# A two-block transformer kernel on one core: the second block's residual held as rows, quadrant products with row norms, smaller units and another start in the first block

## The chip, the cores and the metric

The kernel runs on one core of a Trainium2 chip. The metric is the device time of one execution in microseconds (us); smaller is better. A core has a matrix engine (TensorE, in the rows PE, its weight loads PEld), a vector engine (VectorE, DVE), a scalar engine (ScalarE, ACT), GpSimd (POOL) and SyncE (SP), which here issues the transfers of weights. All data are float32. Matrix results land in eight PSUM banks of 128 partitions by 512 values (`bank[0]` to `bank[7]`); everything else lives in SBUF.

## The reference

Two transformer blocks of depth 2 run one after the other on 256 tokens of width 1024.

```python
# first block, each of 2 layers
proj = x @ w_in[l]                       # q, k, v, conv gates cb cc and input cu, qm, branch gates
y_attn = diff_attention(rope(q), rope(k), v, lam, lam_init, diff_subln_g[l])
y_conv = cb * conv3(cc * cu, conv_w[l])  # short_gated_conv
y_mem  = memory_attention(qm, mem, w_mem_kv[l])     # kv = mem @ w_mem_kv
merged = g0*(y_attn @ w_br_attn) + g1*(y_conv @ w_br_conv) + g2*(y_mem @ w_br_mem)
x = layer_norm(ALPHA * x + merged @ w_out[l]);  x = layer_norm(ALPHA * x + grouped_moe(x))

# second block, each of 2 layers; layer 0 updates 256 context tokens too
h = rms_norm(x, g_mix[l]) * (1 + sc1) + sh1          # the same with ctx and its own sc, sh, gt
o = [global_attention, fourier_mix, window_attention](h @ w_in_2[l])
x = x + gt1 * (o @ w_out[l])                         # first output projection
x = x + gt2 * swiglu(rms_norm(x, g_ffn[l]) * (1 + sc2) + sh2, w_gate, w_up, w_down)
return rms_norm(x, g_final)
```

What the change computes in another order are `y_conv @ w_br_conv`, `mem @ w_mem_kv`, the start, and in the second block's layer 0 `o @ w_out`, `... @ w_down`, both gated residual sums and the two root-mean-square norms behind them.

## The kernel before, in words

Each engine has a program of its own, written by hand; semaphores connect them. SP loads weights as tiles of 128 x 4096 values (2 MB) into six slots of `ring`, in the order in which TensorE uses them; a slot is loaded again when TensorE has released it. In SBUF an activation lies mostly as *features* (feature on partition, token along it: `X`, `h2`, `ff`); a *row* layout has tokens on partitions.

**Units.** Several products use seven multiplications of quadrants where a plain product has eight (Strassen's scheme in Winograd's form). A `unit` (before L621) does this for 256 tokens by two weight tiles: TensorE makes seven quadrant products into banks 0 to 6; ScalarE copies the first (`first_product`), VectorE makes the sums of weight quadrants in place in `ring` (`tile_sum`, L1951) and adds the products up. `seven_products` does the same for the second block's layer 0 in feature layout, gate/up (11 units) and down (4 units of 11 by 256 columns), with x in the first 256 columns and the context in the last 256. There `sums_but_last`, `last_sum` and `down_sums` make the weight sums.

**Start.** SP issues x, mem and ctx and then waits for all small parameters (25 transfers that ScalarE's queue issues) before it issues the first weight tile. TensorE waits for all of this too, turns x, mem and ctx into features (48 transposes at L921, copies by ScalarE at L1600), turns the parameters (L925 to L927) and then waits for the sines and cosines that VectorE and ScalarE make (`s_tables`, DVE L2115), before its first product.

**First block, before the attention.** Tiles 0 to 3 (q, k) in features with rope on VectorE, a unit for v, tiles 6 and 7 (conv gates, copied by ScalarE at L1508), tile 8 (conv input), a unit for a branch gate, then `token_blocks(cbT)` (16 matmuls of 512 columns), `tile_features(memT)` (32 of 256 columns) and `token_product(memT)` (16 of 512), and tile qm. Then the attention steps.

**Second block, layer 0, after the attention.** The output projection makes eight feature chunks of 8 matmuls with 512 columns (x and context together). VectorE adds each to `X` with its gate (L2815), ScalarE squares it (L1696), and TensorE adds up the squares with a matrix of constants (`square_step`, `mean_d`), each chunk's one product later. Then the norm: VectorE and ScalarE make the root and its reciprocal for 256 columns of 128 equal rows, VectorE scales (L2424), ScalarE modulates (L1712), and gate/up begins. The down units end in the same kind of chain, into layer 1's first projection (L2379, L1703). In layer 1 the late part already works with rows: `X` is turned back into rows `xt` (L688 on `X`), a diagonal of the gate times a matrix of ones spreads the gate over all rows (`gate_diag`, `gain_rows`), and `late_rows_turned` turns normed rows back into features.

## Time and profile before

| | us |
|---|---|
| median of 3 runs | 2390.91 (2390.05 to 2396.14) |
| profiled execution | 2389.61 |
| its span, first to last instruction | 2387.9 |
| TensorE busy | 2255.7 (94%) |
| VectorE busy | 1104.1 (46%) |
| ScalarE busy | 440.7 (18%) |
| mean granted TensorE clock | 0.979 of full |

The chain that ended last is TensorE's for 78% of the span, DMA's for 8% (experts) and VectorE's for 8%. One float32 matmul instruction of the program shows in the trace as two records (a transpose as one), so a row `x16` of 512 columns is eight matmuls; a record's duration overlaps with the next one, so the pace is read from start to start.

### The profile page before, as it was taken

Reading aid. Unit: us, or ns where it says so; the run is one execution under the profiler, and the core shown is the slowest. Engines: PE = TensorE matmul, PEld = TensorE weight load, DVE = VectorE, ACT = ScalarE, POOL = GpSimd, SP = SyncE. Lnnn points to the kernel's source line nnn. Section 1 sums busy time; section 2 is a strip of 40 time slices with the busy share of each in tenths; the row PEclk is TensorE's granted clock in tenths of the full one; section 3 lists DMA queues with packets and bytes.
Section 4 is the critical chain, followed back from the end, with each engine's and each line's share of the span. In section 5 each row is a group of like instructions: output and inputs, shape, how many; then the busy total and the mean of one; then the engine's idle time right before and its main releaser. Section 6 shows DMA issues by size and latency. Waiting matters only on the chain.

```text
span 2387.9 us, 24216 instructions
## 1 busy us (share of the span) xinstructions
PE 2255.7 (94%) x9653; PEld 1394.4 (58%) x9653; DVE 1104.1 (46%) x1902; ACT 440.7 (18%) x969; POOL 3.5 (0%) x23
## 2 busy tenths in 40 slices
PE   5999899999989998999999998899999998998998
PEld 4776444544456764445444585548888886654453
DVE  3631666311157316663111338525556533577675
ACT  1000421211111004112111215421000002352010
POOL 0000000000000000000000000000000000000000
PEclk8999999899999999998999998999999999999999
DMA  7344943599972449435999610001221215113340
GB/s 300 115 176 176 385 179 141 217 423 427 428 301 106 176 176 378 186 141 209 417 428 428 259 71 36 1 0 71 79 99 62 105 64 211 71 45 127 147 167 18
DMA packets 34925, 450.34 MB, mean 189 GB/s; under 512 B 5128, under 2 KB 6010, under 8 KB 7418
## 3 DMA queue, kind: packets, MB, share of 16 engines
q1 hardware_dynamic: 32208, 447.63, 46.1%
q10 hardware_dynamic: 2602, 1.12, 0.2%
q8 instruction: 80, 1.31, 0.2%
q14 instruction: 35, 0.29, 0.0%
HBM read 447.68 MB, written 1.05 MB: 188 GB/s over the span
## 4 chain that ended last, share of the span: by engine, by line
PE 78%; DMA 8%; DVE 8%; DVEq 2%; issue 1%; ACT 1%; ACTq 0%; SPq 0%
PE banks L531 75%; DMA ring<-in_w_exp_up 8%; PE banks L1425 1%; DVE tiny L2784 1%; DVE arena L1928 1%; DVEq L1929 1%; PE banks L688 1%; PE banks L1005 0%; DVE arena L2801 0%; DVE arena L1917 0%; DVE ring L1951 0%; DVE tiny L2174 0%; PE banks L921 0%; ACT arena L1703 0%; DVE arena L2188 0%
## 5 line engine op out<-in xcount | busy, mean ns | idle before, releaser
L531 PE MATMUL banks<-ring,arena 128*64 128x512 f32 (+2 forms) x2642 | 807.5, 590 | 16.9 <-DMA ring<-in_w_exp_up 6.8
L531 PEld LDWEIGHTS banks<-ring,arena 128*64 128x64 f32 (+1 forms) x2642 | 320.1, 159 | 473.7 <-issue 460.0
L531 PE MATMUL banks<-arena,ring 128*128 128x256 f32 (+1 forms) x1040 | 278.1, 424 | 12.1 <-ACT arena L1703 7.6
L531 PE MATMUL banks<-arena 128*128 128x128 f32 (+6 forms) x1616 | 252.1, 349 | 11.9 <-DVEq L2769 3.9
L531 PEld LDWEIGHTS banks<-arena,ring 128*128 128x128 f32 x1040 | 198.4, 192 | 86.4 <-issue 59.1
L531 PE MATMUL banks<-X,ring 128*128 128x256 f32 x1024 | 225.7, 383 | 12.0 <-DVEq L2115 11.5
L531 PEld LDWEIGHTS banks<-X,ring 128*128 128x128 f32 x1024 | 196.5, 192 | 41.6 <-issue 14.4
L531 PEld LDWEIGHTS banks<-arena 128*128 128x128 f32 (+2 forms) x1616 | 164.5, 181 | 83.8 <-issue 36.1
L2049 DVE TENSOR_TENSOR arena<-arena,banks 128x512 f32<-128x512 f32 x16 | 11.0, 688 | 265.6 <-ACT arena L1583 265.6
L531 PE MATMUL banks<-arena,wsums 128*128 128x256 f32 x528 | 118.9, 379 | 0.0
L531 PE MATMUL banks<-ring 128*128 128x256 f32 x528 | 118.5, 379 | 0.0
L531 PE MATMUL banks<-ring,X 128*128 128x512 f32 x256 | 113.1, 593 | 0.4 <-ACT wsums L1508 0.3
L531 PEld LDWEIGHTS banks<-arena,wsums 128*128 128x128 f32 x528 | 100.3, 190 | 13.6
L531 PEld LDWEIGHTS banks<-ring 128*128 128x128 f32 x528 | 100.3, 190 | 13.6
L2581 DVE TENSOR_TENSOR ring<-ring 128x2048 f32<-128x2048 f32 (+2 forms) x40 | 85.3, 2132 | 32.5 <-PE banks L531 14.7
L1951 DVE TENSOR_TENSOR ring<-ring 128x2048 f32<-128x2048 f32 x40 | 91.6, 2290 | 13.4 <-ACT arena L1545 9.2
L531 PEld LDWEIGHTS banks<-ring,X 128*128 128x128 f32 x256 | 48.3, 190 | 59.5 <-issue 58.4
L1508 ACT ACTIVATE arena<-banks 128x256 f32<-128x256 f32 (+1 forms) x72 | 31.5, 442 | 265.5 <-PE banks L531 264.4
L2174 DVE TENSOR_REDUCE tiny<-banks 128x2 f32<-128x512 f32 (+1 forms) x40 | 23.4, 584 | 94.7 <-PE banks L531 92.0
L531 PE MATMUL banks<-ring,wsums 128*128 128x256 f32 x264 | 60.3, 380 | 3.6 <-DVEq L2435 1.9
L1928 DVE RECIPROCAL arena<-arena 128x512 f32<-128x512 f32 (+1 forms) x21 | 59.1, 2815 | 2.2 <-ACT arena L1516 1.3
L2032 DVE TENSOR_TENSOR arena<-arena,banks 128x512 f32<-128x512 f32 x64 | 43.9, 686 | 33.7 <-PE banks L531 33.7
(331 smaller groups left out, 1874.3 us busy)
## 6 DMA issues: line engine op xcount, KB each, us to landing
ring<-in_w_in SPq DMA_DIRECT2D x38, 2048.0 KB, 9.4
ring<-in_w_exp_gate SPq DMA_DIRECT2D x32, 2048.0 KB, 13.5
ring<-in_w_exp_up SPq DMA_DIRECT2D x32, 2048.0 KB, 16.6
ring<-in_w_exp_down SPq DMA_DIRECT2D x32, 2048.0 KB, 12.0
ring<-in_w_ada SPq DMA_DIRECT2D x24, 2048.0 KB, 9.6
ring<-in_w_ffn SPq DMA_DIRECT2D x22, 2048.0 KB, 7.5
ring<-in_w_out SPq DMA_DIRECT2D x8, 2048.0 KB, 12.5
ring<-in_w_down SPq DMA_DIRECT2D x8, 1408.0 KB, 6.2
```

The lines of the kernel that those rows point to most:

```text
L531: ins = nc.tensor.matmul(out, weights, moving, start=start, stop=stop)
L688: ins = nc.tensor.transpose(bank[b][:, i * P:i * P + P], s_, ident[:])
L1425: ins = nc.tensor.transpose(banks[:, TURNED + par, k * P:k * P + P], probs2[s % 2][:, par, k * P:k * P + P], ident[:])
L1508: done(fn(dst, take()[:, 0:n], func, scale=scale))
L1928: v.reciprocal(dst, dst)
L1929: drain()
L1951: tt(out_, a, b, ALU.subtract)
L2032: done(tt(part_, part_, bank[(7, 4)[i % 2]][:], ALU.add))
L2049: tt(hid, sig1, bank[0][:], ALU.mult).then_inc(s_gate_read, 1)
L2174: v.tensor_reduce(tiny[:, o:o + 2], banks[:, b:b + 2, 0:n * P], AX_X, ALU.max, negate=True) .then_inc(s_max, 1)
L2581: tt(out_, a_, b_, sub)
L2784: ins = v.tensor_reduce(tiny[:, o:o + 2], banks[:, b:b + 2, 0:n * P], AX_X, ALU.max, negate=True)
```

## The change

1. **Start.** SP issues x, the two conv gate tiles (6 and 7), then mem and ctx, then waits for the parameters (23 now; positions and frequencies come first in ScalarE's queue under `s_turns`). TensorE turns x (copied by VectorE), multiplies tiles 6 and 7 in layer 0 at once, and only then turns the parameters, mem and ctx. The waits for the tables are gone from TensorE (VectorE makes and uses them); the wait `s_cond` stands ahead of the attention.
2. **First block.** The conv projection is a unit with `kh=2` (one tile), mem's keys and values one unit of two tiles; the keys come out as rows and are turned by 8 transposes (`turned_keys`), half of them ahead of the unit's last product, half after tile qm.
3. **Second block, residual.** At the end of layer 0's input projection 16 transposes turn x into rows (`XR`, a view of `X`); SP loads the context's rows from the input once more. In layer 1 these transposes are gone.
4. **Output projection and down, layer 0.** `row_unit`: two units each, tokens as the stationary operand, 256 weight columns as the moving one, seven products of 2 x `kh` matmuls (`kh` is 4 and 11). VectorE gates a result with a row of gains (`row_gained`: multiply by `gain_rows`, add to `XR`). The gains come from ScalarE (`gain_diags`, 16 copies of `ident`) and TensorE (`gain_row`, 4 matmuls of 512 columns): for the output projection during the expert routing of the first block's layer 1, for down inside its first unit.
5. **Norms.** ScalarE squares and sums along a row, root and reciprocal are one value per row, VectorE and ScalarE scale one half of the features each, TensorE turns them (`rows_turned`, 4 transposes per half and row block), and both engines modulate while copying out of PSUM (`row_chunks`). All matmuls with `mean_d` over squares of `X` in these two places are gone.

TensorE's order at the very start, before and then after (`wsums` holds the loaded x, `arena` mem, ctx and the parameters, `X` x as features, `ident` the transposes' identity):

```order
L921 MATMUL banks<-ident,wsums 128x128 x16
L921 MATMUL banks<-ident,arena 128x128 x32
L925 MATMUL banks<-ident,arena 128x104
L926 MATMUL banks<-ident,arena 128x96
L927 MATMUL banks<-ident,arena 128x46
L531 MATMUL banks<-X,ring 128x256 x128
```

```order
L966 MATMUL banks<-ident,wsums 128x128 x16
L549 MATMUL banks<-X,ring 128x256 x64
L978 MATMUL banks<-ident,arena 128x104
L979 MATMUL banks<-ident,arena 128x96
L980 MATMUL banks<-ident,arena 128x46
L966 MATMUL banks<-ident,arena 128x128 x32
L549 MATMUL banks<-X,ring 128x256 x128
```

The 64 matmuls of tiles 6 and 7 stand ahead of the parameters' and of mem's and ctx's transposes.

TensorE's order from the second block's output projection into gate/up, before (the end of it) and after (all of it; L787 and L794 are `rows_turned`, `arena` holds `h2`, the normed rows and, after, the first unit's weight sums):

```order
L531 MATMUL banks<-arena,ring 128x512 x8
L531 MATMUL banks<-arena,mean_d 128x512
L531 MATMUL banks<-arena,ring 128x512 x8
L531 MATMUL banks<-arena,mean_d 128x512 x2
L531 MATMUL banks<-arena,ring 128x256 x16
L531 MATMUL banks<-ring,wsums 128x256 x8
```

```order
L549 MATMUL banks<-ring,arena 128x256 x112
L787 MATMUL banks<-ident,arena 128x128 x4
L794 MATMUL banks<-ident,arena 128x128 x4
L787 MATMUL banks<-ident,arena 128x128 x4
L794 MATMUL banks<-ident,arena 128x128 x4
L549 MATMUL banks<-arena,ring 128x256 x16
L787 MATMUL banks<-ident,arena 128x128 x4
L794 MATMUL banks<-ident,arena 128x128 x4
L787 MATMUL banks<-ident,arena 128x128 x4
L794 MATMUL banks<-ident,arena 128x128 x4
L549 MATMUL banks<-ring,arena 128x256 x8
```

64 matmuls of 512 columns and 8 over squares became 112 of 256; 16 transposes stand ahead of gate/up and 16 behind its first two products.

TensorE's order at the end of down and the start of layer 1's input projection, before and after:

```order
L531 MATMUL banks<-ring 128x256 x11
L531 MATMUL banks<-arena,wsums 128x256 x11
L531 MATMUL banks<-arena,mean_d 128x512 x4
L531 MATMUL banks<-arena,ring 128x256 x24
L531 MATMUL banks<-arena,ring 128x512 x16
```

```order
L549 MATMUL banks<-ring 128x256 x44
L787 MATMUL banks<-ident,arena 128x128 x4
L794 MATMUL banks<-ident,arena 128x128 x4
L787 MATMUL banks<-ident,arena 128x128 x4
L794 MATMUL banks<-ident,arena 128x128 x4
L549 MATMUL banks<-ring,arena 128x256 x22
L549 MATMUL banks<-arena,ring 128x256 x24
L787 MATMUL banks<-ident,arena 128x128 x4
L794 MATMUL banks<-ident,arena 128x128 x4
L787 MATMUL banks<-ident,arena 128x128 x4
L794 MATMUL banks<-ident,arena 128x128 x4
L549 MATMUL banks<-arena,ring 128x512 x16
```

x is turned ahead of the last product (22 matmuls), the context ahead of the fourth chunk of layer 1.

```diff
-UNIT_AT = (4, 9, 27, 30, 32)
+UNIT_AT = ((6, 9, 11, 12, 27, 30, 32), (4, 9, 11, 12, 27, 30, 32))
+FIRST_TILES = ((6, 7, 0, 1, 2, 3, 4, 5, 8, 12, 13), (0, 1, 2, 3, 4, 5, 6, 7, 8, 12, 13))
-DOWN_SLOTS = (2, 0, 1, 5)
+DOWN_PLACES = ((2, 0, 1, 5), (2, 1, 5, 0))
+X_BANKS, CTX_TURN_BANKS = ((7, 0), (3, 2)), ((7, 6), (3, 2))
...
+                for i, c in enumerate(FIRST_TILES[l]):
+                    if l == 0 and i == 2:
+                        for n in ("mem", "ctx_2"):
+                            sp.dma_start(raw[n], ...).then_inc(s_inputs, 16)
+                        sp.wait_ge(s_params, PARAM_DMAS * 16)
                     tile(block_of("w_in", l * 16 + c))
...
-                token_blocks(cbT)
-                tile_features(memT, T, "act")
-                token_product(memT)
+                unit(cbT, conv_sums, summed=ROWS_SUMMED * l + 2, kh=CC // 2)
+                unit(memT, mem_sums, summed=ROWS_SUMMED * l + 3, last_but_one=lambda: turned_keys(0))
                 tile_features(X, T, "act")
+                turned_keys(1)
...
+            def row_unit(weights, tokens, sums, kh, ...):        # TensorE
+                product(0, x_[:, lo, :], ll, lo_ready).then_inc(s_full["act"], 1)
+                handed(product(1, x_[:, hi, :], hl, hi_ready), 1, 1)
+                if after_second: after_second()                   # down, unit 0: gain_row
+                if sums_ready: sums_ready()
+                handed(product(2, t4, hh), 2, 4)
+                if after_fourth: after_fourth()                   # down, unit 0: gain_row
+                weight_sums(1)
+                handed(product(3, c_[:, lo, :], ll), 3, 3)
+                if each_used: each_used()
+                weight_sums(2)
+                handed(product(4, t2, hh), 4, 2)
+                weight_sums(1)
+                if each_used: each_used()
+                handed(product(5, t1, lh), 5, 5)
+                if each_used: each_used()
+                if after_fifth: after_fifth()                     # down, unit 1: rows_turned
+                handed(product(6, c_[:, hi, :], hl), 6, 6)
+                used()
...
+            def row_gained(j, q, gains, y):                       # VectorE
+                tt(y2, y2, gain, ALU.mult)
+                r = XR[:, :, q, j * T:j * T + T]
+                tt(r, r, y2, ALU.add)
+            def row_unit(u, weights, gains, loaded=None, ...):    # VectorE
+                dve.wait_ge(s_first, C.next("first"))
+                tt(ll, ll, lh, ALU.subtract); tt(lh, lh, hh, ALU.add)
+                filled(); tt(y, first_p, bank[1][:], ALU.add); row_gained(0, 2 * u, gains[0], y)
+                filled(); tt(hh, hh, ll, ALU.subtract); tt(hl, hl, hh, ALU.subtract)
+                if filler: filler()
+                filled(); filled()
+                tt(u_two, first_p, bank[4][:], ALU.add); tt(u_three, u_two, bank[3][:], ALU.add)
+                tt(y, u_three, bank[2][:], ALU.add); row_gained(0, 2 * u + 1, gains[0], y)
+                if x_done: drain().then_inc(s_late_rows, 1)
+                filled(); tt(y, u_three, bank[5][:], ALU.add); row_gained(1, 2 * u + 1, gains[1], y)
+                tt(u_two, u_two, bank[5][:], ALU.add)
+                if x_normed: x_normed()
+                filled(); tt(u_two, u_two, bank[6][:], ALU.add); row_gained(1, 2 * u, gains[1], u_two)
...
-            for c in range(DC):                                   # VectorE and ScalarE, before
-                tt(hx[:, c, :], X[:, c, 0:T], root2[:, 0:T], ALU.mult).then_inc(s_scaled, 1)
-                x_ = h2[:, c, j * T:j * T + T]; fn(x_, x_, ACT.Identity, scale=gmod[...], bias=ada[...])
+            def rows_normed(j, rows):                             # ScalarE
+                    fn(rows[TC * j + tc], XR[:, tc, :, j * T:j * T + T], ACT.Square, accum_out=moments[:, tc, 0:1])
+                fn(rstd[:].unsqueeze(2), moments[:, :, 0:1], ACT.Sqrt, scale=1.0 / D, ...)
+                    fn(rows[TC * j + tc][:, 0:2, :], XR[:, tc, 0:2, ...], ACT.Copy, scale=rstd[:, tc:tc + 1])
```

## Rows read from the trace of the kernel before

**Rows 1.** Waits of PE: who waited for whom, us in total, times, longest.

```profile
PE banks L921 <- DMA invf<-in_inv_freq: 16.1, 1, 16.1
...
PE banks L531 <- DVEq L2115: 11.5, 1, 11.5
```

**Rows 2.** Windows: length, PE, PEld, DVE, ACT, POOL busy, clock, DMA share, GB/s.

```profile
37.40:43.80 6.40, 6.35 (x17) 5.18 (x18) 0.01 (x1) 0.00 (x0) 0.00 (x0) 0.58 0.99 421
...
185.30:226.70 41.40, 41.39 (x129) 24.44 (x130) 3.26 (x5) 3.29 (x7) 0.00 (x0) 1.00 0.52 203
```

**Rows 3.** DMA issues: KB each, median us from issue to landing.

```profile
wsums<-in_x SPq DMA_DIRECT2D x1, 1024.0 KB, 5.0
...
ring<-in_w_down SPq DMA_DIRECT2D x8, 1408.0 KB, 6.2
```

**Rows 4.** Timeline, start: start us, us, engine, line, what [idle before, releaser].

```profile
15.96 38.94 SPq L376 DMA_DIRECT2D ring<-in_w_in  x7
...
24.47 1.15 PE L921 MATMUL banks<-ident,arena 128*128 128x128 f32 x8 [0.19 <-ACT X L1600]
...
37.45 24.86 PE L531 MATMUL banks<-X,ring 128*128 128x256 f32 x102 [11.48 <-DVEq L2115]
```

**Rows 5.** Timeline, first block: a weight sum, a 512-wide sum, the attention's first matmul.

```profile
170.66 7.11 DVE L1951 TENSOR_TENSOR ring<-ring 128x2048 f32<-128x2048 f32 x3
...
181.76 0.69 DVE L1977 TENSOR_TENSOR arena<-arena,banks 128x512 f32<-128x512 f32 x1 [3.98 <-PE banks L531]
...
241.21 1.10 PE L531 MATMUL banks<-arena 128*128 128x256 f32 x4 [0.57 <-ACT arena L1508]
```

**Rows 6.** Timeline, second block, output projection into gate/up.

```profile
1535.37 14.00 PE L531 MATMUL banks<-arena,ring 128*128 128x512 f32 x32
...
1538.29 1.23 DVE L2397 TENSOR_TENSOR wsums<-ring 128x1024 f32<-128x1024 f32 x1
...
1550.07 7.03 PE L531 MATMUL banks<-arena,ring 128*128 128x512 f32 x16
...
1602.71 8.78 PE L531 MATMUL banks<-arena,ring 128*128 128x256 f32 x32 [4.18 <-ACT arena L1712]
...
1617.48 3.62 PE L531 MATMUL banks<-arena,wsums 128*128 128x256 f32 x16
...
1620.94 7.07 PE L531 MATMUL banks<-ring 128*128 128x256 f32 x32
```

**Rows 7.** Timeline, layer 1's late part: a row norm as the change uses it.

```profile
2161.31 1.06 ACT L1752 ACTIVATE arena<-wsums 128x1024 f32<-128x1024 f32 x1 [17.46 <-DVEq L2641]
...
2162.54 0.29 ACT L1754 ACTIVATE rstd<-moments,tiny 128x1 f32<-128x1 f32 x1
...
2165.66 0.60 PE L1225 MATMUL banks<-ident,arena 128*128 128x128 f32 x4
2166.30 1.50 ACT L1765 ACTIVATE arena<-banks,ada,gmod 128x128 f32<-128x128 f32 x4 [1.01 <-PE banks L1225]
```

**Rows 8.** Timeline, down: its start, a product, its end, layer 1.

```profile
1873.03 9.66 PE L531 MATMUL banks<-arena,ring 128*128 128x256 f32 x44
...
2001.89 4.91 PE L531 MATMUL banks<-ring 128*128 128x256 f32 x22
2006.64 4.91 PE L531 MATMUL banks<-arena,wsums 128*128 128x256 f32 x22
...
2021.85 4.62 PE L531 MATMUL banks<-arena,ring 128*128 128x256 f32 x10 [6.87 <-ACT arena L1703]
...
2029.38 0.38 ACT L1508 ACTIVATE arena<-banks 128x256 f32<-128x256 f32 x1 [0.79 <-PE banks L531]
```

**Rows 9.** Timeline: `X` turned in layer 1, PE's wait in layer 0, the routing.

```profile
1096.88 0.61 PE L531 MATMUL banks<-arena,before 128*128 128x16 f32 x2 [3.03 <-DVEq L2293]
...
1442.52 2.08 PE L531 MATMUL banks<-arena 64*128 64x512 f32 x4 [3.89 <-DVEq L2769]
...
2059.36 1.29 PE L688 MATMUL banks<-ident,X 128*128 128x128 f32 x8
```

More of the change, by code:

```diff
@@ L1367, in _ @@
                 release()
+                if l == 0:
+                    for i, b in enumerate((2, 3, 6, 7)):
+                        transposes([X[:, 4 * (i % 2) + j, (i // 2) * P:(i // 2) * P + P] for j in range(4)], b, "act")
                 def channels(i):
@@ L2235, in _ @@
                 branch = lambda tc, half: ((unit_done, unit_two), (unit_three, unit_first))[tc][half]
-                unit(UNIT_SLOTS[l][2], rows(gates), more=(head_variances,),
+                unit(UNIT_SLOTS[l][4], rows(gates), more=(head_variances,),
                      filler=(lambda: head_norm(0), lambda: head_norm(1)))
```

890 lines of the change are left out of this document (506 added, 384 removed).

## The prediction

> **What bounds the kernel now.** I first read the table of times: TensorE is busy for 2255.7 of 2387.9 us, no other engine for half of that. Only two things shorten such a kernel, fewer matrix columns and shorter idle stretches of TensorE. Next the waits of TensorE: the two longest single ones are at the start, 16.1 us for the last small parameter and 11.5 us for the rope tables [rows 1]. Then the windows for its clock: 0.58 of full in the first 6.4 us of real work, that is mostly 1.2 GHz after the idle time before it, and 1.00 (2.4 GHz) in the stretch of the conv and memory projections [rows 2]. Last the timeline of the places that the diff touches. The pace there: 16 records of 512 columns stand as 7.03 us, 32 of 256 columns as 7.07 [rows 6], both with some 0.2 us of the last record's tail; 22 records of 256 take 4.75 from start to start (2001.89 to 2006.64 [rows 8]). A matmul is two records, so 256 columns cost 0.43 us and 512 cost 0.85: per column the width makes no difference. Four transposes are 0.60 us [rows 7].
>
> The experts' stage is supplied by DMA at its end, but its loads start when TensorE releases slots; what is saved ahead of it moves both.
>
> **Start.** Before, TensorE begins its first product at 37.45, loses 6.35 - 17 records x 0.213 = 2.7 us to the clock [rows 2, 4], and at about 40.2 has all tiles ahead. After: x needs 5.0 us from its issue at 0.8 [rows 3]; 16 transposes and four VectorE copies, alternating in two banks at some 0.9 us, end near 10.5. The conv gate tile (2 MB) stands behind x's 1 MB; seven tiles are issued from 15.96 on and the stretch runs at 421 GB/s [rows 2, 4], so 3 MB need about 7.5 us and a latency: 11.8 us. First product at 11.8; tiles 6 and 7 are 64 x 0.427 = 27.3 us and lose the same 2.7 to the clock: 41.8. Then 3 parameter and 32 more transposes, 8 per 1.3 us with copies of ScalarE beside them (24.47 and 1.15 long [rows 4]): 6 us, so tile 0 starts at 47.8. With tiles 6 and 7 done, that is a start at 20.5 against 40.2: **-19.7**, of which I count 19. Hidden: the tables (VectorE works beside tiles 6 and 7), mem and ctx (7 MB by some 20 us), the parameters, which have until 41.8, tile 0 until 47.8.
> The Trainium skill ("DMA: Bandwidth & Descriptors", section on queues, rings and completion order) says that an engine takes turns between queues packet by packet. By that rule ScalarE's small loads get their turn beside SP's 7 MB and don't stand behind them; the sum is then as above. No row shows these small loads beside so much.
>
> **First block, per layer.** The conv product goes from 16 to 14 matmuls of 512 columns (-1.7 us), mem from 32 of 256 and 16 of 512 (27.3) to 28 of 512 (23.9), plus 8 transposes (1.2). The seams: in the conv unit the quadrant products last only 1.7 us. VectorE's sum of 1024 columns is 1.23 us, a 512-wide sum 0.69 [rows 5, 6]; the first sum ends 3.9 us after the unit's start where TensorE wants it at 5.1, the second at 6.7 against 6.8, the later ones earlier than needed. In mem's unit VectorE comes at 19.3 us from the evictions and gates of the conv unit, its first sum of 2048 columns (2.3 us) ends at 21.6, TensorE wants it at 22.2. So no stall, with margins of 0.1 and 0.6 us; if VectorE is later by 2 us, each layer loses 2 to 3. Sum: 41.0 becomes 36.9, **-4.1 per layer, -8.2**. The last turned key is copied by ScalarE ahead of the attention as qm's last chunk was (0.57 us idle [rows 5]).
>
> **Output projection.** Before: 1535.4 to 1602.7, then the context's chain until gate/up's fourth product at 1617.48 [rows 6]. After: 112 x 0.427 = 47.8 us for the products. VectorE first makes four activation sums (4 x 1.3, ready at 1541.1; TensorE wants the first at 1542.3), then per unit four weight sums (5.2), about 16 operations of 512 columns (11 to 12) and in unit 0 the gate/up sums (5.2) and modulation (1.1). It ends unit 0 at 1564.4, when TensorE is 4.9 us into unit 1, whose first sum is wanted at 1569.8: it fits. x's rows are complete 4 us after product 4 (1576.7), at 1580.7. The norm in layer 1's late part is the pattern: square 1.06 per row block, root 0.29, then reciprocal, scaling, turning 0.60, modulation 1.50 per row block and half [rows 7]. With two row blocks: 1583.7 for the root, first transposes 1585, gate/up at 1588.3, where the last projection product ended at 1583.3. The context follows behind the first two gate/up products (to 1595.2): transposes 2.4, modulation 3, and the sums per chunk 1.0 us each, so the fourth product starts at 1605.1. **-12.4**: 11.3 from columns, 1.1 from the seam.
>
> At this place a rule speaks against the change. The rows give 0.213 us per record of 256 columns and twice that for 512 [rows 6]. The Trainium skill ("TensorE: Matmul & The Clock Gate", section on the back-to-back issue gap) gives 81 ns sustained for 128 columns and 131 ns for 512, so that narrow matmuls are dearer per column. On a straight line between the two, 256 columns cost half as much again per column as 512; by that estimate the output projection's 47.8 us would be 24 more, and the gain there a loss of 12. The trace doesn't agree for float32 and decides.
>
> **Down.** 308 matmuls of 256 columns both times, a product of 22 records is 4.75 us [rows 8] and one of a row unit 9.5. From 1873.03 to the end of layer 1's first chunk it takes 156.2 us before (2029.2, 0.2 ahead of ScalarE's copy) [rows 8]. After: 14 x 9.5 = 133, gain rows 3.4 (4 matmuls of 512; ScalarE's diagonals are ready 13 us in, wanted at 19). VectorE's weight sums are 2816 columns, 3.3 us each; the tiles that it waits for land within 6.2 us of a release [rows 3], about 10 us in, and are wanted from 30 on: hidden. New is a stall: `rows_turned` stands behind product 5, but VectorE scales x only behind product 5's three evictions and gains: 2.9 us, reciprocal, scaling 0.5: TensorE is idle 4.1 us, then turns 2.4. x's modulation is hidden by product 6, so the first chunk ends at 133 + 3.4 + 6.5 + 3.4 = 146.3: -9.9. Then the context: rows ready 7 us behind product 6, turned ahead of the fourth chunk 10.2 us behind it, 2.4 and 0.6 us for transposes and modulation: -3.0 back. **-6.9**.
>
> **The rest.** The 16 transposes in layer 1 cost two stretches of 1.29 us and vanish: **-2.6**; in layer 0 they fall into TensorE's wait of 3.89 us for VectorE and cost nothing (up to 2.6 if not) [rows 9]. The gain matmuls in the routing (3.4 us) fall into a wait of 3.03 [rows 9]: **+0.6** with their copies; ScalarE's 16 diagonals, about 5 us, lie beside the first block's output product.
>
> Sum: -19 - 8.2 - 12.4 - 6.9 - 2.6 + 0.6 = -48.5. The profiled execution took 2389.61 and would be 2341.1; the median is 1.3 above it: 2342.4. I take **2343 us**.
>
> **Rivals.** (a) VectorE becomes the bound in the row units. For: its operations get strided and spread operands that no row shows, and margins are 0.1 to 5 us. Against: it is busy 46%. Bounds: the same 0.69 us, or twice that; doubled, 8 gain operations in each of 4 units are 5.5 us a unit, of which the chains at the two unit ends show fully (2 x 5.5) and some 4 in the conv units: 2358. (b) The start gains half: a parameter or tile 0 lands 10 us late, or the clock stays at 1.2 GHz through tiles 6 and 7's transposes: 2353. (c) Row products with 256 moving columns are slower than those of the rows, since tokens are now the stationary operand and each load serves half as many columns: a record of 0.32 us instead of 0.213 in the output projection is 47.8 x 0.5 = +24: 2367. Against: gate/up and down run 256 columns at full pace with a load each [rows 6, 8]. (The page's rule above is this case.) (d) Slower: in the down units the eight tiles of 1408 KB come when they are wanted, not before. Place: product 0 to 2 of each unit; price: 6.2 us each to land and 3.3 for the sum behind it, 8 x 9.5 = 76: 2419. It decides from 6.1 us per tile (48.5 / 8). Against: slots are released after products 3, 4, 5 and 6, the first three 9 to 28 us ahead of use. (e) The change doesn't do what it says: seams as long as before and only the columns' net (6.8 us) and the start's 19 are gained: 2365.
>
> **How the numbers follow.** Forecast 0.67 (its own range 2334 to 2351), (a) 0.13, (b) 0.09, (c) 0.02, (e) 0.04, (d) 0.02, and 0.03 for a mixture that ends within 0.3% (7 us, about what a measurement of this kernel can tell from no change). The margin below is small, since the columns are fixed: 2333; above it reaches over (a): 2360. Faster 0.95, same 0.03, slower 0.02.
>
> **What would show it.** TensorE's first product of 256 columns near 12 us and tile 0 near 48; the attention of layer 0 some 23 us earlier than 241.2; 47.8 us of row products after the heads, gate/up 5 us behind them; a wait of 4 us ahead of the last down product; none on a ring tile in down. Wrong would be: VectorE named in TensorE's waits inside row units, a granted clock under 0.9 in them, or a first product later than 16 us.

## The result and the profile after

| | before | after |
|---|---|---|
| median in us | 2390.9 (4 runs, 2390.05 to 2396.14) | 2348.7 (4 runs, 2345.36 to 2353.9) |
| ratio | | 0.9827 (0.9812 to 0.9843) |
| profiled execution, its span | 2389.61, 2387.9 | 2345.36, 2343.6 |
| mean granted TensorE clock | 0.979 | 0.984 |

The change makes the kernel 1.7% faster: 42 us by the medians, 44.3 by the spans of the two profiles. Forecast were 2343 us, 47.9 below the median before, and the terms of the sum give 48.5. Five more runs of the same kernel, timed later beside others, gave 2352.9 (2346.5 to 2353.63; 0.9842, 0.9829 to 0.9856). The executions of the changed kernel lie up to 8 us apart, and both of its profiles are at the lower end; why is shown below, for one place. First the engines on the page after (busy us, share of the span, instructions): TensorE is busy for 23.6 us less, VectorE for 83 more.

```profile
PE 2232.1 (95%) x9725; PEld 1396.9 (60%) x9725; DVE 1186.9 (51%) x1984; ACT 451.3 (19%) x1013; POOL 3.5 (0%) x23
```

and TensorE's waits after (who waited for whom, us in total, times, longest):

```profile
PE banks L966 <- DMA wsums<-in_x: 8.7, 1, 8.7
PE banks L549 <- issue: 7.4, 9, 2.4
PE banks L549 <- DMA ring<-in_w_exp_up: 6.2, 11, 1.0
PE banks L787 <- DVE arena L2581: 5.0, 2, 3.9
PE banks L549 <- DVEq L2710: 3.4, 3, 2.6
```

The two long waits at the start [rows 1] are gone. New are 8.7 us for x, L787 (the new turning of rows) and a longer "issue". To see where the time went, take the same instruction in both timelines and subtract. The last column is the prediction's running sum.

| TensorE reaches | before | after | moved by | forecast |
|---|---|---|---|---|
| attention, layer 0 | 241.21 | 217.72 | -23.5 | -23.1 |
| first expert product, layer 0 | 447.00 | 423.90 | -23.1 | -23.1 |
| last scatter, layer 0 | 676.74 | 655.73 | -21.0 | -23.1 |
| attention, layer 1 | 898.86 | 874.43 | -24.4 | -27.2 |
| first expert product, layer 1 | 1105.55 | 1078.57 | -27.0 | -26.6 |
| last scatter, layer 1 | 1335.37 | 1309.45 | -25.9 | -26.6 |
| output projection | 1535.37 | 1509.67 | -25.7 | -26.6 |
| gate/up's fourth product | 1617.48 | 1580.58 | -36.9 | -39.0 |
| head sums of layer 1 | 2049.82 | 2007.57 | -42.3 | -45.9 |
| attention of layer 1, second block | 2091.59 | 2046.43 | -45.2 | -48.5 |
| end of the span | 2387.9 | 2343.6 | -44.3 | -48.5 |

The rows after, as those of before stand in rows 4 to 6 and 8 (start us, us, engine, line, what, [idle before, releaser]). The start:

```profile
8.74 3.84 PE L966 MATMUL banks<-ident,wsums 128*128 128x128 f32 x16 [8.74 <-DMA wsums<-in_x]
13.83 7.14 PE L549 MATMUL banks<-X,ring 128*128 128x256 f32 x32 [1.24 <-DMA ring<-in_w_in]
21.98 20.99 PE L549 MATMUL banks<-X,ring 128*128 128x256 f32 x96 [1.01 <-ACT arena L1590]
...
48.24 51.97 PE L549 MATMUL banks<-X,ring 128*128 128x256 f32 x240
...
217.72 1.10 PE L549 MATMUL banks<-arena 128*128 128x256 f32 x4 [0.95 <-ACT arena L1728]
```

The first product is 2 us later than predicted (13.8 for 11.8), tile 0 is not (48.2 for 47.8). The products wait once more, at 21.98, for ScalarE (third row). But they lose nothing to the clock: all of the first 128 records ran at full pace (32 in 7.14 us, 96 in 20.99), where the forecast had 2.7 us of loss. With the wait of 1.0 us they took 29.0 us, against 30.0 forecast.

The output projection into gate/up:

```profile
1509.67 48.61 PE L549 MATMUL banks<-ring,arena 128*128 128x256 f32 x224
1559.38 0.66 PE L787 MATMUL banks<-ident,arena 128*128 128x128 f32 x4 [1.09 <-DVE arena L2581]
...
1562.50 7.14 PE L549 MATMUL banks<-arena,ring 128*128 128x256 f32 x32 [1.16 <-ACT arena L1835]
...
1574.04 0.67 PE L549 MATMUL banks<-ring,arena 128*128 128x256 f32 x2 [2.65 <-DVEq L2710]
...
1580.58 3.62 PE L549 MATMUL banks<-arena 128*128 128x256 f32 x16
```

One row holds all 224 records of the two row units: no wait among them, 0.216 us from one to the next, the pace of [rows 6]. Gate/up follows 4.4 us behind the last (1562.50 against 1558.1), for 5.0 forecast. Then the context's chain, with 3.4 us of waits, takes 18.1 us to the fourth product for 16.8 forecast.

Down, and layer 1's first projection:

```profile
1836.13 19.16 PE L549 MATMUL banks<-ring,arena 128*128 128x256 f32 x88
...
1954.82 8.37 PE L549 MATMUL banks<-ring 128*128 128x256 f32 x38
1967.13 0.66 PE L787 MATMUL banks<-ident,arena 128*128 128x128 f32 x4 [3.95 <-DVE arena L2581]
...
1969.30 10.97 PE L549 MATMUL banks<-ring,arena 128*128 128x256 f32 x44
1980.11 10.74 PE L549 MATMUL banks<-arena,ring 128*128 128x256 f32 x48
...
1993.76 13.97 PE L549 MATMUL banks<-arena,ring 128*128 128x512 f32 x32 [1.16 <-ACT arena L1835]
```

The predicted stall ahead of the last down product is there: 3.95 us for 4.1. The product behind it takes 10.8 us to the next start instead of 9.5, which the forecast lacked; the granted clock was 0.64 in its first 3.7 us and 1.00 behind them.

The routing of layer 1, before and after (the first selection in both is `x32` of 128 columns), and the scatter behind the experts' stage:

```profile
1099.56 6.05 PE L531 MATMUL banks<-arena 128*128 128x128 f32 x32 [0.36 <-issue]
...
1335.37 3.01 PE L531 MATMUL banks<-arena 128*128 128x256 f32 x8 [0.73 <-issue]
```

```profile
1067.73 5.30 PE L549 MATMUL banks<-arena,ones 128*128 128x512 f32 x8 [0.29 <-ACT arena L1590]
...
1074.83 3.81 PE L549 MATMUL banks<-arena 128*128 128x128 f32 x32 [0.77 <-issue]
...
1309.45 5.37 PE L549 MATMUL banks<-arena 128*128 128x256 f32 x10 [2.34 <-issue]
```

The gain rows (4 matmuls, `x8`) took the place of the wait of 3.03 us [rows 9]. Behind them the same 32 selection records take 3.81 us instead of 6.05; the granted clock in them was 1.00 after and 0.60 before. And at the scatter TensorE is idle 2.34 us, where it was 0.73: a wait for nothing that the profile shows.

### The profile page after: what moved, and what is told of

Same layout as the page of the kernel before. It is cut to its first block, busy times and chain, and to the rows that moved or that the text cites. A ratio compares the mean times of both kernels' runs of the same rounds, so it can differ in the third digit from the quotient of the medians.

```text
span 2343.6 us, 24658 instructions
## 1 busy us (share of the span) xinstructions
PE 2232.1 (95%) x9725; PEld 1396.9 (60%) x9725; DVE 1186.9 (51%) x1984; ACT 451.3 (19%) x1013; POOL 3.5 (0%) x23
## 4 chain that ended last, share of the span: by engine, by line
PE 77%; DMA 10%; DVE 8%; DVEq 2%; issue 1%; ACT 1%; ACTq 1%; SPq 0%
PE banks L549 74%; DMA ring<-in_w_exp_up 10%; PE banks L1524 1%; DVE tiny L2976 1%; DVEq L2053 1%; PE banks L700 1%; DVE arena L2052 1%; PE banks L1064 0%; DVE arena L2041 0%; DVE arena L2993 0%; DVE ring L2078 0%; DVE tiny L2324 0%; DVE arena L2338 0%; DVE banks L2321 0%; PE banks L739 0%
## 5 line engine op out<-in xcount | busy, mean ns | idle before, releaser
L549 PE MATMUL banks<-ring,arena 128*64 128x512 f32 (+2 forms) x3322 | 979.9, 554 | 19.7 <-DMA ring<-in_w_exp_up 6.2
L549 PEld LDWEIGHTS banks<-ring,arena 128*128 128x128 f32 (+1 forms) x3322 | 451.6, 166 | 516.6 <-issue 482.6
L549 PE MATMUL banks<-arena,ring 128*128 128x256 f32 (+1 forms) x736 | 178.0, 398 | 2.4 <-ACT arena L1835 2.3
L549 PEld LDWEIGHTS banks<-arena,ring 128*128 128x128 f32 x736 | 139.3, 190 | 36.6 <-issue 17.3
L549 PE MATMUL banks<-ring 128*128 128x256 f32 x616 | 137.0, 379 | 0.0
L2078 DVE TENSOR_TENSOR ring<-ring 128x2048 f32<-128x2048 f32 (+1 forms) x56 | 119.7, 2138 | 18.0 <-ACT arena L1634 12.4
L549 PE MATMUL banks<-ring,X 128*128 128x512 f32 x192 | 85.1, 593 | 0.3 <-ACT wsums L1590 0.3
L549 PE MATMUL banks<-arena,wsums 128*128 128x256 f32 x320 | 72.3, 379 | 0.0
L549 PEld LDWEIGHTS banks<-arena,wsums 128*128 128x128 f32 x320 | 60.8, 190 | 8.3
L1590 ACT ACTIVATE arena<-banks 128x256 f32<-128x256 f32 (+1 forms) x60 | 25.9, 439 | 163.2 <-PE banks L549 162.3
L2268 DVE SCALAR_TENSOR_TENSOR arena<-banks,sinT 32x256 f32<-32x256 f32 x128 | 53.8, 421 | 1.7
## 6 DMA issues: line engine op xcount, KB each, us to landing
ring<-in_w_exp_down SPq DMA_DIRECT2D x32, 2048.0 KB, 11.8
```

What stands on the lines that cost most here:

```text
L549: ins = nc.tensor.matmul(out, weights, moving, start=start, stop=stop)
L1590: done(fn(dst, take()[:, 0:n], func, scale=scale))
L2078: tt(out_, a, b, ALU.subtract)
L2268: ins = stt(tmp2[o], b[i, 0:T], scale, sinT[i], ALU.mult, ALU.mult)
```

## The experiments

All start from the changed kernel. Differences "on the timeline" are those of the same instruction in the two profiles, as in the table above; of medians I use only what is beyond the spread of some 8 us, unless their intervals are named. No run undoes the row units and row norms (items 3 to 5 of the change) by themselves: what these gave is read from the two timelines, between the same instructions.

**1. The order of the loads alone undone** (SP only):

```diff
+            for n in ("mem", "ctx_2"):
+                sp.dma_start(raw[n], ...).then_inc(s_inputs, 16)
+            sp.wait_ge(s_params, PARAM_DMAS * 16)
...
-                    if l == 0 and i == 2:
-                        for n in ("mem", "ctx_2"): ...
-                        sp.wait_ge(s_params, PARAM_DMAS * 16)
```

> The changed kernel, but SP issues x, mem and ctx first and waits for all parameters before the first ring tile, as before; the order of TensorE's products stays the new one. It splits the start's gain (19.5 us on the timeline) in two. Theory A (the early tiles matter as much as the new order of products): the first tile is issued at some 16 us and lands near 22, so the first product of 256 columns starts at 22 to 24 instead of 13.8; everything behind follows 8 to 10 us later: about 2357 us, attention of layer 0 near 227. Theory B (the order of the products is the whole gain, because x, mem, ctx and the parameters share the DMA engines with the tiles in either order): the first product at under 17 us and no more than 3 us lost: 2349 to 2352.

Measured: 2359.7 (2359.28 to 2363.12), 0.9866 (0.9842 to 0.9889), 11 us above the changed kernel. The first product starts at 24.70, with 12.2 us of idle time named after the ring tile, and the attention of layer 0 is 12.4 later. So of the start's 19.5 us some 12 come from the early tiles and the rest from the order of products: theory A, a little more than expected (8 to 10 us).

**2. Less beside x** (one wait more on SP):

```diff
+                    if l == 0 and i == 1:
+                        sp.wait_ge(s_x, 16)
                     tile(block_of("w_in", l * 16 + c))
```

> The changed kernel, but SP issues the second ring tile only when x has landed (one wait more). Theory A (x and the two first tiles, 5 MB, share the DMA engines, so that each lands late): x lands near 7 instead of 8.7, the first tile near 10 instead of 13.8, the first product starts at 11.5 to 12.5 instead of 13.8, as the prediction had it; tile 2 is needed only 13.8 us later and its 2 MB take about 5, so nothing waits for it: 1.5 to 2 us less than the changed kernel, 2344 to 2347. Theory B (transfers of one queue finish in the order of their issue, the 8.7 us are x's own time beside the parameters' small loads): x at 8.7 and first product at 13.8 as they are, no change of the time.

Measured: x lands at 8.72, as in the changed kernel, and the first product starts at 13.96. Theory A fell for x. "Nothing waits" fell too: the third product starts at 23.33 (it waits for ScalarE, see experiment 3), its 96 records take 22.65 us instead of 20.99, and the attention comes 3.0 us later, for 2349.4 (2348.91 to 2351.25). The second ring tile isn't what holds x. In experiment 1 no ring tile was issued beside x at all, and x landed at 8.61: it isn't the first one either.

**3. Positions and frequencies later in ScalarE's queue**:

```diff
-            act.dma_start(pos_i, a["positions"]...).then_inc(s_turns, 16)
-            act.dma_start(invf[:], a["inv_freq"]).then_inc(s_turns, 16)
             for st, r0, n, src in rows:
                 act.dma_start(st[r0:r0 + n, :], src).then_inc(s_params, 16)
+            act.dma_start(pos_i, a["positions"]...).then_inc(s_turns, 16)
+            act.dma_start(invf[:], a["inv_freq"]).then_inc(s_turns, 16)
```

> The changed kernel, but ScalarE issues the positions (128 KB to 128 partitions) and the frequencies behind the eight blocks of small parameters instead of first. x landed 5.0 us from its issue before, 7.8 in the changed kernel, 7.7 when SP's order was that of before and 7.8 with one ring tile less beside it: what all of these three have and before has not is these two loads in front of ScalarE's. Theory A (they hold back x): x lands near 5.8 instead of 8.7, the first product starts at 10.9 to 12 instead of 13.8, everything behind follows by 2 to 3 us. Theory B (the engines are at their rate in any case and x only shares it): x at 8.7 and no gain.

Measured: x's load after, then with this edit (KB, us from issue to landing), and TensorE's rows with the edit:

```profile
wsums<-in_x SPq DMA_DIRECT2D x1, 1024.0 KB, 7.8
```

```profile
wsums<-in_x SPq DMA_DIRECT2D x1, 1024.0 KB, 4.9
```

```profile
5.86 3.84 PE L966 MATMUL banks<-ident,wsums 128*128 128x128 f32 x16 [5.86 <-DMA wsums<-in_x]
11.18 10.18 PE L549 MATMUL banks<-X,ring 128*128 128x256 f32 x32 [1.48 <-DMA ring<-in_w_in]
22.27 20.99 PE L549 MATMUL banks<-X,ring 128*128 128x256 f32 x96 [0.91 <-ACT arena L1590]
```

Two small loads on ScalarE's queue, one of them 128 rows of 4 bytes, cost x 2.9 us. The Trainium skill ("DMA: Bandwidth & Descriptors", section "Issuing engines are not separate DMA queues") has the queues of all engines share the same DMA engines, and the trace agrees, in that loads of ScalarE's queue delay one of SP's. It calls the time to issue a DMA "usually small relative to the DMA itself"; of the rows below one issue took 2.98 us and one, of 0.1 KB, 5.49. The first product now starts at 11.2, near my 11.8 (its 32 records take 10.18 us and not 7.14, since the first 14 stand 0.43 us apart, as at half the clock), but the third still waits to 22.27. Nothing is gained behind it: the attention is 0.3 us later, 2350.3 (2346.71 to 2353.34) beside 2352.9 of the changed kernel in the same group. Both banks are full, and ScalarE, which empties them, is still issuing (its queue in the changed kernel):

```profile
11.71 2.98 ACTq L1575 DMA_DIRECT2D wr<-in_w_router  x1
14.73 5.49 ACTq L1576 DMA_DIRECT2D rbias<-in_router_bias  x1
20.25 1.28 ACT L1590 ACT_TABLE_LOAD   x1 [20.25 <-issue]
```

So what bounds tiles 6 and 7 is ScalarE's list of small loads, until 20.2 us, and the load of its table behind it. The list alone isn't that long. In experiment 1 SP's ring tiles waited for the parameters, and the same list (25 transfers) was issued by 12.3 us:

```profile
11.37 0.46 ACTq L1574 DMA_DIRECT2D wr<-in_w_router  x1
11.85 0.46 ACTq L1575 DMA_DIRECT2D rbias<-in_router_bias  x1
12.34 1.28 ACT L1589 ACT_TABLE_LOAD   x1 [12.34 <-issue]
```

In experiment 2 the last issue took 9.71 us, until 21.6. SP loads x, mem and ctx beside the list in each of these; what makes the difference of 8 to 9 us are the two ring tiles in its queue. The prediction had assumed that small loads get their turn beside them. Theory A was right on x and wrong on what follows.

**4. The first block's two small units undone** (`token_blocks(cbT)`, `tile_features(memT)`, `token_product(memT)` put back on TensorE, with ScalarE's copies and VectorE's products with the gates as before):

```diff
-                unit(cbT, conv_sums, summed=ROWS_SUMMED * l + 2, kh=CC // 2)
-                unit(memT, mem_sums, summed=ROWS_SUMMED * l + 3, last_but_one=lambda: turned_keys(0))
+                token_blocks(cbT)
+                tile_features(memT, T, "act")
+                token_product(memT)
                 tile_features(X, T, "act")
-                turned_keys(1)
```

> The changed kernel with the conv and the memory projections of the first block as before (16 matmuls of 512 columns for conv, 32 of 256 and 16 of 512 for memory), in both layers; all else is the changed kernel. Theory A (the two small units gain what their columns say, 4.1 us per layer less 0.1 to 0.7 at their seams): attention of layer 0 starts 4.0 us later than 217.7, that of layer 1 7.4 later than 874.4, and the whole is 7 to 8.5 us slower than the changed kernel, about 2356. Theory B (what is gained ahead of the experts' stage is lost in it, since its loads run at the DMA engines' rate of 428 GB/s from its third pair on): the attention starts as much later, but behind each experts' stage the difference is under 1.5 us per layer and the whole is under 4 us slower: 2349 to 2353.

Measured on the timeline: attention of layer 0 later by 4.5, first expert product by 4.3, last expert product by 4.6, attention of layer 1 by 7.8, the end by 8.0; median 2354.0 (2350.57 to 2357.32), 0.9843 (0.9816 to 0.987). Theory A. The experts' stage takes nothing of it away (behind it the difference is 2.9, because the branch of experiment 5 costs 1.7 less in this kernel), although TensorE waits in it for `w_exp_up`: its loads start when TensorE releases slots, and these moved too. Layer 1's block alone, from the scatter to the attention, is longer by 4.9 us (223.6 for 218.7), and other kernels with the changed code lie up to 1.1 us above that 218.7. The median is 5.3 us above the changed kernel's, which is within the spread.

**5. TensorE without its branch** behind the experts' stage (the overflow rounds, which these inputs never take, are left out of its program):

```diff
-                more = pe.value_load(rounds_i[0:1, 0:1])
-                with pe.If(more >= 1):
-                    last_scatter()
-                    ...
-                with pe.Else():
-                    ...
-                    last_scatter()
+                last_scatter()
```

> The changed kernel, but TensorE has no branch behind the experts' stage: the overflow rounds, which these inputs never take, are left out of its program, and the last scatter stands in line. It asks what the 2.40 and 2.34 us ahead of the last scatter are (0.73 in each layer before), which the profile puts down to nothing. Theory A (they are the branch: reading the register, jumping, and fetching the code at its target): both fall under 0.5 us, 4 us in all: about 2345. Theory B (they are a wait for work of another engine that the records don't show): they stay, and the time does.

**6. TensorE's program 16 instructions longer at the start**:

```diff
+            for _ in range(16):
+                pe.wait_ge(s_ones, 1)
```

> The changed kernel with 16 more instructions in TensorE's program at its start, waits on a semaphore that has long been reached. It asks what sets the idle time at TensorE's branch (0.73 us before, 2.40 and 2.34 after). Theory A (the position of the code at the jump's target decides how long its fetch takes): the idle time is another one than 2.4 in both layers, by up to 1.7 us each, and nothing else moves: 2345 to 2349. Theory B (it depends on how busy the DMA engines are, or on the other engines): 2.3 to 2.4 in both layers, no change of the time.

Measured: without the branch the row of the first fence, 0.73 us and the same in layer 1, and 2342.0 (2338.39 to 2346.55). With 16 instructions more the rows of the second, 2349.4 (2344.99 to 2353.67):

```profile
652.78 3.01 PE L549 MATMUL banks<-arena 128*128 128x256 f32 x8 [0.73 <-issue]
```

```profile
655.20 3.01 PE L549 MATMUL banks<-arena 128*128 128x256 f32 x8 [2.39 <-issue]
...
1311.65 3.01 PE L549 MATMUL banks<-arena 128*128 128x256 f32 x8 [0.73 <-issue]
```

Theory A in both, but not as far as expected: 0.73 us stay without a branch (under 0.5 expected), so that is the seam itself, and the 16 instructions took the extra away in layer 1 alone and left it in layer 0 (expected was a change in both). The branch costs nothing or 1.0 to 2.2 us more. In the eight profiles whose TensorE program is the changed kernel's up to the branches, the wait is 2.40 to 2.91 us in layer 0 and 1.74 to 2.90 in layer 1; in the three with instructions added (experiments 6, 7 and the third edit) 2.35 to 2.39 and 0.73; before and with the small units undone 0.73 in both.

What TensorE waits for stands among the DMA records of the traces: loads of instructions, of 16 KB each, on a queue of their own (`q8 instruction` in section 3 of a profile page). Around the last scatter (us from the span's start):

| kernel, layer | such a load ends | first scatter record | later by | idle before |
|---|---|---|---|---|
| changed, 0 | 654.16 | 655.73 | 1.57 | 2.40 |
| experiment 2, 0 | 658.17 | 659.75 | 1.58 | 2.91 |
| changed, 1 | 1307.79 | 1309.45 | 1.66 | 2.34 |
| experiment 9, 1 | 1313.64 | 1315.30 | 1.66 | 1.74 |
| experiment 6, 1 | 1308.23 | 1311.65 | 3.42 | 0.73 |
| experiment 7, 1 | 1304.37 | 1307.71 | 3.34 | 0.73 |

In all 19 cases with the longer wait TensorE goes on 1.56 to 1.67 us after such a load has ended, while the idle time varies from 1.74 to 2.91: it waits for that load. In five of the seven cases of 0.73 us with a branch the load ended 2.8 to 3.4 us ahead of the scatter, early enough; in the other two (layer 1 before, and with the small units undone) the last one ended under 0.3 us ahead, and the idle time is that of the seam, so nothing waited for it. Without the branch none ends in the 14 us before the scatter. The Trainium skill ("Runtime: NRT & Kernel Launch", section on instruction fetch mechanics) says that a taken branch whose target isn't among the pages at hand must fetch it by DMA. The traces agree, in that there is such a load to wait for at the branch. That the load comes early or late by the position of the code is what experiment 6 shows; how it is decided no run shows.

**7. Products in layer 0's routing** (their results are read by nobody):

```diff
                 free(5)
+                if l == 0:
+                    for k in range(4):
+                        mm(bank[5][:], ones[:], X[:, k, :], start=True, stop=True)
                 pe.wait_ge(s_chosen, C.next("chosen"))
```

> The changed kernel with four more matmuls of 512 columns, whose results nobody reads, in layer 0's routing, where TensorE waits for VectorE's choice of experts (in layer 1 the gain rows stand there now). Theory A (TensorE's idle time there brings its clock down to 1.2 GHz, and busy it stays at 2.4): the 32 selection records of layer 0 take 3.8 us instead of about 6, the first experts' products start 2 to 2.7 us earlier. What of it arrives behind the stage depends on the loads: I expect under 1 us, because TensorE waits for w_exp_up from the second pair on; the whole within 1 us of the changed kernel. Theory B (the shorter selection in layer 1 comes from something else, e.g. earlier operands): the four matmuls change nothing or cost up to 1 us, selection stays near 6 us.

Measured, the selection of layer 0 after and with this edit:

```profile
418.21 5.76 PE L549 MATMUL banks<-arena 128*128 128x128 f32 x32 [0.36 <-issue]
```

```profile
419.16 3.81 PE L549 MATMUL banks<-arena 128*128 128x128 f32 x32 [0.76 <-issue]
```

and the windows of these records (length, PE, PEld, DVE, ACT, POOL busy, clock, DMA share, GB/s):

```profile
418.00:423.90 5.90, 5.69 (x33) 5.60 (x33) 5.41 (x11) 0.59 (x1) 0.00 (x0) 0.64 0.01 3
```

```profile
419.20:422.90 3.70, 3.70 (x33) 3.58 (x33) 3.33 (x9) 0.58 (x1) 0.00 (x0) 1.00 0.02 4
```

The same 2 us as in layer 1: with work in the place of 3.0 us of idle time the granted clock behind it is 1.00 and not 0.64. But the products also push the selection back by 1 us, 1.0 us is left at the first expert product and 1.6 at the scatter. The median was 2342.5 (2341.75 to 2344.43), 6 us lower. Its profile ends 3.6 us earlier than the changed kernel's, but not by the selection: layer 1's branch waits 0.73 us instead of 2.34, and from the last scatter to the output projection, where the profiles of kernels with the same code lie up to 5 us apart, it takes 197.5 us for 200.2. See also experiment 10.

**8. VectorE's weight sums in down made twice**:

```diff
+                def again(a_, b_):
+                    for i in range(5):
+                        tt(u_two, a_[:, 2i:2i+2], b_[:, 2i:2i+2], ALU.subtract)
+                        drain()
...
+                again(ll, lh)          # and ahead of each of the other three sums
                 tt(ll, ll, lh, ALU.subtract)
```

> The changed kernel, but in the two down units VectorE does each of its eight weight sums twice (the copy goes to a scratch tile, 2560 of the 2816 columns, some 3.4 us each, 27 us of VectorE's time in all). Theory A (VectorE has that much room in the row units; TensorE's columns are the bound): at most 2 us more than the changed kernel, and a wait on a weight sum only at the unit's first or second. Theory B (rival a of the prediction, VectorE is at its limit in the row units): 8 to 20 us more, with waits of TensorE on the sums in both units.

Measured: 2349.1 (2346.91 to 2350.61), the changed kernel's time. From gate/up's fourth product to the head sums it is 1.2 us slower, none of it in a wait on a sum: 1.3 are the 16 transposes behind the stall of 4 us, at 1.06 us per four instead of mostly 0.60, which is again the clock. VectorE did 27 us more work in down and TensorE waited for none of it. Rival (a) is refuted for these units.

**9. x's rows turned behind the last down product**:

```diff
-                if after_fifth:
-                    after_fifth()
                 handed(product(6, c_[:, hi, :], hl), 6, 6)
                 used()
+                if after_sixth:
+                    after_sixth()
```

and on VectorE x's modulation (`row_chunks`) behind that product too.

> The changed kernel, but in the second down unit the rows of x are turned behind the seventh product instead of the sixth, and VectorE's share of their modulation stands behind the seventh product too. Theory A (the 3.95 us of idle time ahead of the last down product are only the chain product, three sums and gains, root, scaling; any product that stands there hides it, and the last product's 10.97 us instead of 9.5 are the clock after that idle time): no wait above 1.2 us is left there, the last product takes 9.5 us, the first chunk of layer 1 starts 3.5 to 5 us earlier than 1980.1: about 2344. Theory B (VectorE is the bound at this place): the wait moves behind the seventh product or ahead of the context's chunk and under 1 us is gained.

```profile
1968.07 9.66 PE L549 MATMUL banks<-ring,arena 128*128 128x256 f32 x44
1977.57 0.60 PE L787 MATMUL banks<-ident,arena 128*128 128x128 f32 x4
...
1980.65 10.71 PE L549 MATMUL banks<-arena,ring 128*128 128x256 f32 x48 [1.17 <-ACT arena L1835]
```

No stall is left ahead of the last product, it takes 9.5 us, and between gate/up's fourth product and the head sums 4.5 us are gained. 2343.3 (2340.86 to 2345.51), 0.9795 (0.977 to 0.982): theory A.

**10. The changed kernel again, and edits together.** One group on one chip, five runs each.

> The changed kernel once more, beside the three others of this group. Its runs so far spread over 8 us (2345.4 to 2353.9), its profile was at the low end. Theory A (the spread is TensorE's clock: in the attention of layer 1 and the second attention of the layer, where TensorE has short idle times, it is granted 1.2 GHz for some microseconds in some executions and not in others): a median of 2346 to 2350 and a profile whose differences from the first one's timeline sit in those two stages, with the same instructions at twice the time. Theory B (the spread comes from the loads): the differences sit in waits on ring tiles.

> Positions later, and x's rows turned behind the last down product. The second gave 4.2 us on the timeline (from the output projection to the head sums of layer 1) alone. If the two add up: 6 to 7 us less than the changed kernel of this group. A rival: the earlier start is lost in layer 0's experts' stage, where TensorE waits for w_exp_up from the second pair on, and 4 to 5 are left.

> The two edits, and the four unread matmuls in layer 0's routing. Alone these took the selection from 5.76 to 3.81 us, 1.6 us were left at the end of that stage and 0.5 at the attention of layer 1, while its median was 6 us below the changed kernel's. Theory A (what is real is the timeline's 0.5 to 1.6 us, the rest was the chance of its executions): 0 to 2 us less than the two edits. Theory B (the median's 6 us are real, from an effect further down): 4 us or more less than the two edits.

Measured: the changed kernel 2352.9, 0.9842 (0.9829 to 0.9856); two edits 2348.1 (2340.81 to 2349.21), 0.9811 (0.9796 to 0.9826); three edits 2343.5 (2340.51 to 2348.5), 0.9804 (0.979 to 0.9817). Both beat the changed kernel, the two edits by intervals that only just part (0.9826 against 0.9829). It is the turning behind the last product that does it, 4.5 us on the timeline of the two edits between gate/up's fourth product and the head sums; the earlier start adds nothing (attention at 218.06 in both). The third edit can't be told from none: the intervals overlap and its timeline is 2.9 us ahead at the head sums, 1.8 of it from the branch (0.73 us in layer 1 instead of 2.56); at the end 1.2 us are left. How much of experiment 7's six us is chance stays open.

What makes the executions differ can be seen where two kernels have the same program so far. In the changed kernel and in that of experiment 9, here are the same records behind the same wait, and the granted clock there (length, PE, PEld, DVE, ACT, POOL busy, clock, DMA share, GB/s):

```profile
928.46 0.33 PE L1064 MATMUL banks<-ident,arena 128*128 128x128 f32 x1 [1.49 <-DVE arena L2338]
928.75 0.68 PE L549 MATMUL banks<-arena 128*128 128x128 f32 x4
929.37 1.92 PE L549 MATMUL banks<-ring,cond 128*32 128x512 f32 x16
...
928.50:932.50 4.00, 4.00 (x33) 1.80 (x37) 1.63 (x7) 0.67 (x3) 0.00 (x0) 1.00 0.87 371
```

```profile
930.13 0.48 PE L1064 MATMUL banks<-ident,arena 128*128 128x128 f32 x1 [1.48 <-DVE arena L2338]
930.42 1.19 PE L549 MATMUL banks<-arena 128*128 128x128 f32 x4
931.54 3.64 PE L549 MATMUL banks<-ring,cond 128*32 128x512 f32 x16
...
930.50:934.50 4.00, 4.00 (x21) 1.41 (x20) 1.17 (x4) 0.27 (x1) 0.00 (x0) 0.50 0.69 297
```

2.4 GHz in one, 1.2 in the other, behind an idle time of 1.5 us in both. In 6 of the 13 profiles behind this section the second happened; all six need 208.1 to 208.2 us from the attention of layer 1 to its experts, the other seven 203.9 to 204.2 (2.7 us of it here, the other 1.3 in the routing, again at half the clock). By the granted clock other such places lie in the second block's attention. That is theory A on the spread, shown for one place. The profile of the changed kernel itself has the good case, so its -44.3 us may flatter it by some us; the medians' 37 to 42 of the two groups are the fairer number.

## Why the prediction was right or wrong

- **Start, -19:** -19.5. Right in sum by luck, since three errors cancel: x lands at 8.7 and not 5.8 (the loads that were moved to the front of ScalarE's queue, experiment 3), so the first product starts at 13.8 and not 11.8; and the forecast made TensorE free to go on from there, when in truth the third product waits for ScalarE until 22 us, a wait of 1.0 us here, and of 3.7 with the three edits of experiment 10, where the first product starts at 11.24. Against both stand the 2.7 us that I gave the clock: here no such loss came, the granted clock was 1.00. (It came in experiment 3, whose first 14 records stand 0.43 us apart.) Tile 0 starts at 48.2 for 47.8.
- **First block, -8.2:** -7.4 on the timeline (4.0 and 3.4); undone, the two blocks are longer by 4.5 and 4.9 us (experiment 4), so the forecast lies between. The stage's margins of 0.1 and 0.6 us held: no wait on VectorE in the conv unit.
- **"What is saved ahead of the experts' stage moves both":** held. The loads gave back 0.4 us in layer 0 and nothing in layer 1. What the sum lacked is the code: TensorE's wait for instructions at the branch behind the stage cost 1.7 and 1.6 us more (experiments 5 and 6), 3.3 of the 4.2 us by which the profile misses the sum.
- **Gain rows in the routing, +0.6:** the cost was 0.4 (-24.4 to -24.0 at the first `onehot` product), but from there to the first expert product 3.0 us were gained by the clock (-24.0 to -27.0), 2.2 of them in the selection. The sign of the term was wrong, +0.6 for -2.6: I priced the products and not the idle time that they replace.
- **Output projection, -12.4:** -11.2. The columns as forecast (48.4 us for 47.8) and the seam (4.4 for 5.0); the context's chain took 18.1 us for 16.8, with 3.4 us of waits for VectorE's sums.
- **Down, -6.9:** -5.4. The stall of 4.1 was 3.95; mis-sized is the product behind it, 1.3 us longer, part of it at the lower clock (9.5 us again without the stall, experiment 9).
- **Transposes, -2.6:** -2.9. Behind that 0.9 us are lost to the end; other kernels with the same code there have 296.3 to 298.7 us for this stretch (before 296.3, changed 297.2), so nothing is to be explained.
- **The rivals.** (a) refuted in down by experiment 8, and in the output projection by a row of 224 records without a wait; (b) no: the first product starts at 13.8 and the clock is 1.00; (c) refuted by the same row, 0.216 us per record and not 0.32; (d) no wait on a ring tile in down; (e) no: the seams shrank as forecast. (Its 6.8 us were the output projection's columns alone and left out the first block's.)

## What to carry to other kernels

Price a stall twice: the idle time, and the product behind it that begins at half the clock (here 4 us cost 5.2, and moving the work away gave 4.5 back); the reverse holds for products put into a wait. When a transfer or a product is moved to the front, follow what is on every engine's own queue until that point: a load on another queue can delay it, and an engine that is issuing transfers empties no bank. A few added instructions can move a branch's target, so look at the "issue" rows at branches before explaining a difference of a few us by the edit.

## What the runs showed of the hardware

- Idle time ahead of a branch's target depends on the position of the code: 0.73 us or 1.7 to 2.9. In all 19 longer waits TensorE went on 1.56 to 1.67 us after a load of 16 KB of instructions had ended.
- After the same idle time of 1.5 us TensorE goes on at 2.4 GHz in some executions and at 1.2 in others, at the place shown 2.7 us, and 4.0 by the experts.
- Two loads of 128 KB and 0.5 KB beside one of 1 MB took it from 4.9 to 7.8 us.
- A list of 25 small transfers kept ScalarE until 12.3 us with no ring tile beside it, and until 20.2 to 21.6 us beside two of 2 MB; the last issue, of 0.1 KB, took 0.46 us in one case and 5.49 to 9.71 in the others.
